# An eighth group of seven block products in the last pair of output columns of a hybrid attention layer

## The reference, cut to what matters

```python
h = rms_norm(x, norm_g)
proj = h @ w_in                   # 256 x 4096 by 4096 x 12,272
aq, ak, av, ..., cz = split(proj)
y_a = sigmoid(ao) * rms_norm(mlstm(aq, ak, av, ai, af)) * silu(az)        # 1024 columns of y
y_b = sparse_attention(rms_norm(c_q @ wuq), k_b, v_b, ...) * silu(bz)     # 2048 columns
y_c = rms_norm(gated_delta(conv(cqkv), cb, ca)) * silu(cz)                # 1024 columns
y = concatenate([y_a, y_b, y_c])
out = x + y @ w_out                                 # 256 x 4096 by 4096 x 4096
```

## Time and profile before

| what | value |
|---|---|
| time, median of 3 runs | 1515.25 us (1514.6 to 1515.85) |
| time of the profiled execution | 1515.99 us |
| its span, first to last instruction | 1514.1 us |
| TensorE busy | 1509.8 us, 6900 matmuls |
| VectorE busy | 1138.6 us |
| ScalarE busy | 821.5 us |
| granted TensorE clock | 1.00 |

### The profile page before, as it was taken

One profiled execution on the slowest core, in us unless ns is written; L12 is line 12 of the kernel. 1 busy time (PEld: TensorE's weight loads), 2 busy tenths in 40 slices (PEclk: granted clock), 3 DMA queues, 4 the chain that ended last, 5 costly groups with the idle time before them and its releaser, 6 DMA issues.

```text
span 1514.1 us, 19057 instructions
## 1 busy us (share of the span) xinstructions
PE 1509.8 (100%) x6900; PEld 1249.9 (83%) x6900; DVE 1138.6 (75%) x1712; ACT 821.5 (54%) x1100; POOL 367.0 (24%) x612
## 2 busy tenths in 40 slices
PE   9999999999999999999999999999999999999999
PEld 7888888888888887888878888888888888888887
DVE  6889899847769855576579676676557789988894
ACT  6766656587533444554545545544345656555563
POOL 9040131330230040126420254344400112000101
PEclk9999999999999999999999999999999999999999
DMA  9876677976788775558765787798875667696867
GB/s 288 283 238 218 198 250 209 254 225 195 223 252 267 235 221 165 158 184 271 248 203 167 231 248 205 241 277 241 236 244 158 216 217 221 205 263 210 237 228 187
DMA packets 209070, 341.47 MB, mean 226 GB/s; under 512 B 53161, under 2 KB 60632, under 8 KB 208720
## 3 DMA queue, kind: packets, MB, share of 16 engines
q1 hardware_dynamic: 184784, 288.66, 61.2%
q0 software_dynamic: 24144, 51.57, 13.1%
q10 hardware_dynamic: 48, 0.02, 0.0%
HBM read 312.81 MB, written 30.83 MB: 227 GB/s over the span
## 4 chain that ended last, share of the span: by engine, by line
PE 98%; DVE 1%; ACT 0%; issue 0%; DMA 0%; DVEq 0%
PE acc L1289 25%; PE acc L1292 25%; PE acc L1291 25%; PE mix L1292 2%; PE mix L1291 2%; PE mix L1289 2%; PE mix L1305 2%; PE mix L1307 2%; PE mix L1306 2%; PE acc L1305 2%; PE acc L1307 2%; PE acc L1306 2%; PE mix L1398 1%; PE mix L1481 1%; PE mix L1470 0%; PE mix L1391 0%
## 5 line engine op out<-in xcount | busy, mean ns | idle before, releaser
L2021 DVE TENSOR_TENSOR w_lo<-w_raw,w_hi 128x1024 fp32r<-128x1024 f32 (+1 forms) x503 | 604.0, 1216 | 252.8 <-ACT w_hi L1626 247.9
L1626 ACT ACTIVATE w_hi<-w_raw 128x1024 fp32r<-128x1024 f32 (+1 forms) x503 | 522.5, 1049 | 371.8 <-PE acc L1292 277.3
L1289 PE MATMUL acc<-w_hi,op_hi 128*128 128x512 f32 (+1 forms) x1628 | 640.4, 393 | 0.3 <-DVE w_lo L2021 0.3
L1292 PE MATMUL acc<-w_hi,op_lo 128*128 128x512 f32 (+1 forms) x1628 | 633.4, 389 | 0.0
L1291 PE MATMUL acc<-w_lo,op_hi 128*128 128x512 f32 (+1 forms) x1628 | 633.3, 389 | 0.0
L1289 PEld LDWEIGHTS acc<-w_hi,op_hi 128*128 128x128 f32 x1628 | 305.7, 188 | 64.7 <-issue 1.3
L1292 PEld LDWEIGHTS acc<-w_hi,op_lo 128*128 128x128 f32 x1628 | 305.6, 188 | 63.8
L1291 PEld LDWEIGHTS acc<-w_lo,op_hi 128*128 128x128 f32 x1628 | 305.8, 188 | 61.9
L993 POOL DMA_DIRECT2D conv_dram<-y x48 | 30.7, 703 | 165.6 <-DVE y L2112 118.4
L1289 PE MATMUL mix<-w_hi,op_hi 128*128 128x512 f32 (+1 forms) x154 | 59.7, 388 | 0.0
L1291 PE MATMUL mix<-w_lo,op_hi 128*128 128x512 f32 (+1 forms) x154 | 59.7, 388 | 0.0
(11 more groups left out here) (566 smaller groups left out, 1798.8 us busy)
## 6 DMA issues: line engine op xcount, KB each, us to landing
w_raw<-in_w_in_dram SPq DMA_DIRECT2D x367, 512.0 KB, 4.5
w_raw<-in_w_out_dram SPq DMA_DIRECT2D x128, 512.0 KB, 4.7
w_raw<-in_w_in_dram SPq DMA_DIRECT2D x16, 384.0 KB, 3.8
w_raw<-in_a_wuq_dram SPq DMA_DIRECT2D x12, 512.0 KB, 5.8
out_dram<-acc POOLq DMA_DIRECT2D x8, 512.0 KB, 7.0
out_dram<-in_x_dram POOLq DMA_DIRECT2D x7, 512.0 KB, 6.3
conv_dram<-y POOLq DMA_DIRECT2D x48, 64.0 KB, 4.0
y<-conv_dram POOLq DMA_DIRECT2D x48, 64.0 KB, 4.3
```

Source lines behind the costliest of these rows:

```text
L1289: nc.tensor.matmul(o, hi[:, kt, tok], hv[:, i, n0:n1], start=(kt == (kts if late else blk["kts"])[0]), stop=False)
L1292: last_mm = nc.tensor.matmul(o, lo[:, kt, tok], hv[:, i, n0:n1], start=False, stop=(kt == blk["kts"][-1]))
L1626: func(split_ap(w_hi, c), w_raw[:, c % RAW_BUFS, 0:n], ACT.Copy).then_inc(hi_ready, 1)
L2021: vec.tensor_tensor(split_ap(w_lo, c), w_raw[:, c % RAW_BUFS, 0:n], split_ap(w_hi, c).bitcast(F32), ALU.subtract).then_inc(lo_ready, 1)
```

## The change

The third pair (columns 6 and 7) gets an eighth group, at index 15, with its own sums of y (`Y_S`, a place in y for their high part, `s_fifteen`, over the columns of index 5). The orders of the second and third pair are rewritten, and so are the places of the sums of y, of the mLSTM's last steps and of the turning of y.

In the second pair the groups stand at positions 1, 4, 6, 8, 10, 12, 14 before and at 1, 3, 5, 7, 9, 11, 14 after (counted from 0). In the third they stand at 1, 3, 5, 7, 9, 11, 13 before and at 1, 3, 5, 7, 9, 10, 12, 14 after: groups 12 and 13 are neighbours.

```diff
-PAIR_KTS = [[4, 5, 6, 7, 8, 15, 9, 14, 10, 0, 11, 1, 12, 2, 13, 3], [15, 8, 4, 5, 9, 6, 10, 7, 11, 0, 12, 1, 13, 2, 14, 3],
-            [15, 8, 4, 9, 5, 10, 6, 11, 7, 12, 0, 13, 1, 14, 2, 3]]
+PAIR_KTS = [[4, 5, 6, 7, 8, 15, 9, 14, 10, 0, 11, 1, 12, 2, 13, 3], [15, 8, 4, 9, 5, 10, 6, 11, 7, 12, 0, 13, 1, 2, 14, 3],
+            [4, 8, 5, 9, 6, 10, 7, 11, 0, 12, 13, 1, 14, 2, 15, 3]]
 SEVEN = [[0, 1, 2, 3, 4, 5], [0, 1, 2, 3, 4, 5],
-         [8, 9, 10, 11, 12, 13], [8, 9, 10, 11, 12, 13, 14], [8, 9, 10, 11, 12, 13, 14]]
-Y_S = [8, 9, 10, 11, 12, 13, 14]
+         [8, 9, 10, 11, 12, 13], [8, 9, 10, 11, 12, 13, 14], [8, 9, 10, 11, 12, 13, 14, 15]]
+Y_S = [8, 9, 10, 11, 12, 13, 14, 15]
...
-S_PIECES = [(8, 10, 11), (9, 18, 23), (12, 25, 28), (17, 26, 30), (18, 34, 42), (25, 40, 44), (46, 47, 54)]
-A_SLOTS = [(1, 4, 10), (7, 11, 18), (22, 27, 30), (34, 36, 41)]
-YD_SLOTS = [40, 43, 53, 62]
+S_PIECES = [(1, 5, 10), (2, 8, 18), (7, 11, 21), (10, 18, 24), (17, 31, 37), (22, 38, 47), (42, 50, 58), (55, 64, 68)]
+A_SLOTS = [(1, 6, 12), (9, 15, 23), (25, 29, 33), (35, 39, 44)]
+YD_SLOTS = [39, 50, 53, 60]
...
+        _, s_fifteen, _ = region([("y_6", [P, D + 1024], F32), ("s_fifteen", [P, 512], F32R), ("y_7", [P, D - 1536], F32)])
...
-            return s_four[:, i - 8] if i < 12 else s_two[:, i - 12] if i < 14 else s_last[:]
+            return s_four[:, i - 8] if i < 12 else s_two[:, i - 12] if i < 14 else s_last[:] if i < 15 else s_fifteen[:]
```

## The result

The kernel after takes 1519.44 us (median of 7 runs, 1518.56 to 1520.95), the kernel before 1515.25 us (7 runs, 1514.45 to 1516.0). The ratio is 1.0028, with a 95% interval of 1.0019 to 1.0038: 4.2 us slower, where 1.2 us was forecast and the range ended at 1518.3.

The account below looks back on a forecast made before the run. TensorE's count of matmuls was taken to bound the kernel. Terms -0.68 + 0.64 + 0.5 + 0.7 + 0 = +1.2 us, added to the median 1515.25, gave 1516.4 us, range 1514.5 to 1518.3.

Parts of the forecast that it names:

- Part 1: Index 15 of the third pair costs 21 matmuls instead of 24 on TensorE: 0.68 us gained.
- Part 2: VectorE's work in the third pair rises from 70.5 to 75.0 us under TensorE's 81.9: fits, costs nothing by itself.
- Part 3: Third pair, neighbouring groups 12 and 13: TensorE stalls while t_hi waits for group 12's end, 0.64 us.
- Part 4: Second pair's new order: group at position 5 stalls on a load late behind GpSimd's accumulating DMAs, 0.5 us, bounds 0 and 1.0.
- The rival in which a load misses the gap between the bursts: Second pair, group 9's second chunk: a late load pushes its successor into GpSimd's DMA burst, price 4.6 us, 1520.3 us; chance 0.09.
- Part 5: Third pair's last group and GpSimd's DMAs come later, so TensorE waits at the last chunk: 0.7 us, bounds 0 and 1.5.
- Part 6: Moved small steps, mLSTM and turning of y in the first pair: cost 0, bounds 0 to 1 us.
- The forecast of no change: Whole kernel: 1516.4 us, 0.08% more, below the about 0.2% a measurement can tell; chance of same 0.87.
- the 0.10 chance that stood for slower: Whole kernel slower by over 0.2%, from the load-misses-gap rival and a rest of piled-up bounds.
- The signs: Expected in the trace: 3 matmuls fewer, stalls at groups 13 and 10, longer stage wait, last chunk up to 1.5 us late.

Follow-up runs that it names:

- the run without the costs: Kernel after with third stage buffer, third pair's last group at position 13, ScalarE waiting by halves of t_hi, second pair's order of before: 1514.74 us, ratio 0.9996.
- the last experiment: Kernel after with the orders and seven groups of before, leaving the moved small steps and unused sums of y for index 15: 1516.00 us, ratio 1.0004.

## Why the prediction was wrong

- **Part 1, 0.68 us gained.** Right: 6897 matmuls at 0.227 us. It never reached the end of the program, as GpSimd's drain set that.
- **Part 2, VectorE's total fits.** Right for this change: the kernel after has no stall that the total would explain, and in the run without the costs eight groups go by with one stall, behind a late load.
- **Part 3, neighbours 0.64.** Measured 0.71, alone and in the kernel after, and nothing once ScalarE waits by halves. Mechanism and size were right.
- **Part 4, second pair 0.5.** Measured 0.70, and 1.0 with the order alone. The mechanism was right, a load that comes late behind GpSimd's DMAs; the size was within its bounds and too low. I took the 4.36 us between ScalarE's start and the group's from the load that has this place in the kernel before, where the index ahead is a plain one, and it was 4.06 and 3.77. The rival in which a load misses the gap between the bursts did not happen: no wait there is near 4.6 us.
- **Part 5, the end, 0.7.** This is the step that failed, in two ways. As a term it was mis-sized: 1.63 us, above the upper bound of 1.5, because I let the DMAs run faster with fewer weights beside them, and they took 12.5 us from first to second issue, as before. The larger failure is a path that the step left out: it looked only at what GpSimd's chain does to TensorE. The same shift of 5.4 us hits GpSimd's own last addition. It was listed as "all GpSimd DMAs behind it come 4.76 us later", but not followed to the end of the program, where the margin is 1.8 us and not the 3.89 us of the last chunk's split. The prediction's own terms give what this path costs. The last group ends later by 4.76 + 0.64 + 0.5 (the stall of part 4 lies ahead of it too), and less 1.8 that makes 4.1 us, a time of 1519.4. This takes the place of the 1.2 for the whole sum and does not come on top of it: the sum with TensorE's stalls and the one with GpSimd's chain run beside each other, and the larger one counts. Measured were 4.2 us. With the 1.3 us that the step took off for faster DMAs it would have been 2.8 us only, so that part of the reasoning had to go as well.
- **Part 6, the moved steps, 0.** The traces bear it out: no new wait and no lost step up to the second pair. The times alone leave room for 2 us (upper end of the interval in the last experiment).
- **The forecast of no change.** The median lies 0.28% over before, inside the 0.10 chance that stood for slower, and for another reason than the rival that carried that chance. That rival's time, 1520.3 us, comes close by accident.
- **The signs.** At group 13 the distance is 0.82, just over the 0.6 to 0.8 named, and TensorE's waits rise to 3.6 us where some 3 were named. ScalarE's wait for the stage grew by 3.2 us and not by 4 or more.

The row that would have told it is the DRAIN of L328 in the trace of the kernel before. No list of busy time has it; it shows when one asks for each engine's last instructions.

## What to carry to other kernels

Where a change moves work that feeds a last DMA, follow it on every engine to the common end, and write down each engine's margin there. On this kernel GpSimd's last DMA must land 3.8 us before the other engines are through to be free (1513.6 to 1517.4 in the kernel after), so place the last accumulating DMA early, or keep GpSimd off the end. Issuing it early does not do by itself when others are queued ahead of it. A buffer that is waited for whole, though it is used in halves, cost nothing here until two of its users became neighbours; waiting by halves took that stall from 0.71 us to nothing. And a place that waits for a load, like group 10 here, takes back what is saved ahead of it.

## What was not expected of the hardware

- GpSimd's drain at the end lasts 3.54 us in eleven of the twelve traces and 3.46 in the one without the last addition; ScalarE's is 1.49, VectorE's 0.44, SyncE's 0.007 us in the traces of before and after.
- Of three accumulating DMAs of 512 KB in GpSimd's queue, the third took 10.0 us from issue to landing when it was issued before the first had landed, and 5.8 when it was issued 1.5 us after that landing.
- The 61st matmul, up to which the twelve kernels do the same work, starts anywhere from 14.5 to 16.2 us in their traces, and one trace lost another 1.1 us before its program differed. So two spans that are less than 2 us apart say little by themselves; distances within a trace do.
